# Expert weight places, first loads after an expert stage, and a first panel in halves, in a two-block transformer kernel

## What is computed

```python
def moe(h, router, w_gate, w_up, w_down):            # three times in the program
    combine = top-2 weights of each token over 16 experts
    y = 0
    for e in range(16):
        he = silu(h @ w_gate[e]) * (h @ w_up[e])     # 1024 x 512 each
        y = y + combine[:, e:e+1] * (he @ w_down[e]) # 512 x 1024
    return y

x = x + attention and gate branches;  x = x + cross_attention(x, mem);  x = x + moe(rms_norm(x))
for i in range(2):
    shift, scale, gate = split(silu(c) @ ada_w[i, 0] + ada_b[i, 0])
    y = (stick_breaking, retention)[i](x * (1 + scale) + shift)
    x = layer_norm(alpha * x + (1 + gate) * y)
    ... the same with its own ada weights around moe ...
```

## Time and profile before

| | us |
|---|---|
| median of 3 runs (1449.73 to 1451.45) | 1450.96 |
| the profiled execution's own time | 1445.98 |
| its span on the core | 1444.1 |
| PE busy | 1306.9 (91%) |
| DVE / ACT / POOL busy | 571.7 / 432.8 / 407.8 |
| the load queue's packets, share of 16 engines | 77.9% |
| HBM read | 445.38 MB, 309 GB/s over the span |

### The profile page before, as it was taken

How to read it: one execution, slowest core, us unless ns; L and a number is a source line. 1 busy time by engine, 2 the same in 40 slices (tenths; PEclk the granted TensorE clock), 3 DMA queues, 4 the chain that set the end, 5 groups by cost and what they waited for, 6 DMA issues and landing times.

```text
span 1444.1 us, 20713 instructions
## 1 busy us (share of the span) xinstructions
PE 1306.9 (91%) x7694; PEld 809.8 (56%) x7695; DVE 571.7 (40%) x1234; ACT 432.8 (30%) x693; POOL 407.8 (28%) x190
## 2 busy tenths in 40 slices
PE   6999998889899899998889999699998979998985
PEld 6887787543334388776333344299886853343422
DVE  5598555522112243447223222376007062422224
ACT  4554443211111236443111111145445331111110
POOL 5893544100000067151000000169964710000000
PEclk9999999999999999999999999999999999999998
DMA  9565567899999995429499999986635479999962
GB/s 356 198 223 178 190 234 291 364 407 416 426 428 425 397 357 189 175 66 404 186 392 413 426 428 424 391 324 212 224 117 219 160 321 398 415 426 428 425 247 108
DMA packets 96829, 448.05 MB, mean 310 GB/s; under 512 B 8092, under 2 KB 10056, under 8 KB 77384
## 3 DMA queue, kind: packets, MB, share of 16 engines
q1 hardware_dynamic: 93056, 445.87, 77.9%
q10 hardware_dynamic: 3656, 0.57, 0.2%
HBM read 445.38 MB, written 1.05 MB: 309 GB/s over the span
## 4 chain that ended last, share of the span: by engine, by line
PE 62%; DMA 20%; DVE 9%; issue 3%; ACT 3%; POOL 2%; SPq 1%; DVEq 0%; ACTq 0%; POOLq 0%
PE ps L432 61%; DMA ring_hi<-in_moe_w_up 9%; DMA ring_lo<-in_w_up 8%; DMA ring_lo<-in_ada_w 3%; POOL WLO L2604 1%; SPq L1260 1%; DVE Z L2020 1%; DVE Z L2008 1%; DVE Z L2021 1%; DVE Z L2019 1%; DMA ring_lo<-in_w_ckv 1%; PE ps L454 1%; POOL RS L2573 1%; ACT WHI L1403 0%; PE ps L897 0%
## 5 line engine op out<-in xcount | busy, mean ns | idle before, releaser
L2604 POOL TENSOR_TENSOR WLO<-ring_lo,WHI 128x1024 fp32r<-128x1024 f32 (+1 forms) x154 | 376.9, 2464 | 675.2 <-ACT WHI L1403 673.4
L432 PE MATMUL ps<-ring_lo,Z 128*64 128x512 f32 x1328 | 435.4, 603 | 24.0 <-DMA ring_hi<-in_moe_w_up 5.3
L432 PE MATMUL ps<-ring_hi,Z 128*64 128x512 f32 x1072 | 379.7, 605 | 20.2 <-DMA ring_lo<-in_w_up 7.1
L432 PEld LDWEIGHTS ps<-ring_lo,Z 128*64 128x64 f32 x1328 | 137.8, 138 | 226.3 <-issue 208.2
L1403 ACT ACTIVATE WHI<-ring_lo 128x1024 fp32r<-128x1024 f32 (+1 forms) x160 | 166.3, 1049 | 204.5 <-PE ps L432 191.4
L432 PEld LDWEIGHTS ps<-ring_hi,Z 128*64 128x64 f32 x1072 | 116.0, 139 | 154.1 <-issue 139.3
L2271 DVE TENSOR_TENSOR Z<-ps,Z 64x512 f32<-64x512 f32 x48 | 33.1, 689 | 331.9 <-ACT Z L1610 325.4
L1610 ACT ACTIVATE Z<-ps 64x512 f32<-64x512 f32 x48 | 28.4, 591 | 344.2 <-PE ps L432 344.2
L432 PE MATMUL ps<-WHI,HTH 128*128 128x512 f32 x320 | 126.4, 395 | 5.0 <-DVE HTL L2473 1.6
L432 PE MATMUL ps<-WLO,HTH 128*128 128x512 f32 x320 | 125.1, 391 | 0.0
L432 PE MATMUL ps<-WHI,HTL 128*128 128x512 f32 x320 | 125.1, 391 | 0.0
(11 more groups left out here) (297 smaller groups left out, 1704.2 us busy)
## 6 DMA issues: line engine op xcount, KB each, us to landing
ring_lo<-in_ada_w SPq DMA_DIRECT2D x24, 2048.0 KB, 8.9
ring_lo<-in_moe_w_gate SPq DMA_DIRECT2D x22, 2048.0 KB, 15.8
ring_hi<-in_moe_w_up SPq DMA_DIRECT2D x20, 2048.0 KB, 17.5
ring_lo<-in_moe_w_down SPq DMA_DIRECT2D x15, 2048.0 KB, 16.1
ring_lo<-in_w_up SPq DMA_DIRECT2D x14, 2048.0 KB, 18.4
ring_hi<-in_moe_w_down SPq DMA_DIRECT2D x13, 2048.0 KB, 15.5
ring_lo<-in_ret_w_in SPq DMA_DIRECT2D x12, 2048.0 KB, 10.5
ring_hi<-in_w_gate SPq DMA_DIRECT2D x9, 2048.0 KB, 16.5
```

The costliest lines, as they stand in the source:

```text
L432: return nc.tensor.matmul(o, l, r, start=start, stop=stop, skip_group_check=True)
L2604: nc.gpsimd.tensor_tensor(WLO[:, q, 0:size], slot(r)[:, q * size:(q + 1) * size], WHI[:, q, 0:size].bitcast(F32), ALU.subtract).then_inc(S ...
```

## The change

Four parts.

1. In every pair but the first, odd up and even down change places. Before, from pair 2 on, odd up went where the pair before had its odd up, and even down where it had its even down; now odd up goes where its even down was, and even down where its odd up was. In pair 1 odd up, even down and odd down went to pair 0's odd gate, odd up and even down; now they go to its even down, odd gate and odd up. The waits in `slot_left` follow: odd up waits for the downs of the pair before, even down for the odd gate and up. The order of the loads stays.
2. Behind the first and second expert stage the first `ada` panel is loaded ahead of the first dense panel. ACT copies its result first, and splits the dense panel's quarters 0 and 1 before the turned rows and 2 and 3 behind them.
3. `ckv` 0 is loaded in two halves with a semaphore each, and ACT waits for the half that it needs.
4. In `layer_norm` the gate product of the piece (t 1, h 0) stands ahead of the wait for the power of t 0 instead of behind the normalised row.

```diff
     ADA_AFTER = {("in", "gb1"): (0, 1), ("w_out", 0): (2, 3), ("cq", 0): (4, 5, 6), ("co", 0): (7, 8, 9),
-                 ("sb", 0): (10, 11), ("sb", 5): (12, 13), ("sb_out", 1): (14, 15, 16, 17),
-                 ("ret", 0): (18, 19), ("ret", 10): (20,), ("ret", 11): (21,), ("ret_out", 3): (22, 23)}
+                 ("moe", 0): (10,), ("sb", 0): (11,), ("sb", 5): (12, 13), ("sb_out", 1): (14, 15, 16, 17),
+                 ("moe", 1): (18,), ("ret", 0): (19,), ("ret", 10): (20,), ("ret", 11): (21,), ("ret_out", 3): (22, 23)}
...
-        first, odd = s[:6], [s[6]] + s[:5]
-        even = odd[:2] + [s[5]] + odd[3:]
+        first, odd = s[:6], [s[6], s[0], s[1], s[4], s[2], s[3]]
+        even = [s[6], s[0], s[5], s[2], s[4], s[3]]
...
+    first_in = [S("half_even"), landed[place[("ckv", 0), 0][0]]]
+    HALVES_BEFORE = (16, 0)
...
-                load(place[key, 0][0], *src)
+                if key == ("ckv", 0):
+                    to = slot(place[key, 0][0]).rearrange("p (c n) -> p c n", n=512)
+                    for h in range(2):
+                        c = slice(KC // 2 * h, KC // 2 * h + KC // 2)
+                        sp.dma_start(to[:, c], src[0][:, c]).then_inc(first_in[h], 16)
+                else:
+                    load(place[key, 0][0], *src)
...
-                if (a, j) == (1, 1):
+                if (a, j) == (0, 2):
                     blocks(L, e - 1, 1)
...
+                elif (a, j) == (1, 1):
+                    wait_expert_read(L, e - 2, 0, 2)
+                elif (a, j) == (0, 2):
+                    wait_expert_read(L, e - 1, 1, 1)
...
+                else:
+                    act.wait_ge(first_in[q // 2], 16)
...
-            split_next(("sb", 0))
             ada_copy(10)
+            split_next(("sb", 0), parts=(0, 1))
             turn_split("sbx", KC)
+            split_next(("sb", 0), parts=(2, 3))
             ada_copy(11)
...
+            def gated(t, h):
+
+                o = result(dve, (*key, t, h))
+                link(V.tensor_tensor(o, o, GB[:, 512 * h:512 * h + 512], ALU.mult))
+                return o
...
-                rstd(row_moments(t, EPS_LN, False))
+                k = row_moments(t, EPS_LN, False)
+                if t == 0:
+                    gated(1, 0)
+                rstd(k)
```

More of the change, by code:

```diff
@@ L981, in pair @@
                     if final:
-                        pe.wait_ge(S(("half_even", "half_odd")[a]), 32 * (L + 1))
+                        pe.wait_ge(S(("half_even", "half_odd")[a]), HALVES_BEFORE[a] + 32 * (L + 1))
                     for j in range(0 if final else 2):
@@ L1395, in split_next @@
             r, landed_at, _ = place[key, 0]
-            act.wait_ge(landed[r], landed_at)
+            if n:
+                act.wait_ge(landed[r], landed_at)
             size = stream[order.index(key)][1][1] // QUARTERS
@@ L1750, in _ @@
         if ("ret", 0) in order:
-            split_next(("ret", 0))
             ada_copy(18)
+            split_next(("ret", 0), parts=(0, 1))
             turn_split("rx", KC)
+            split_next(("ret", 0), parts=(2, 3))
             ada_copy(19)
@@ L2402, in layer_norm @@
             key = ("sb_out" if s == 0 else "ret_out", "o")
+            def gated(t, h):
+                o = result(dve, (*key, t, h))
+                link(V.tensor_tensor(o, o, GB[:, 512 * h:512 * h + 512], ALU.mult))
+                return o
             for t in range(NT):
                 for h in range(2):
-                    o = result(dve, (*key, t, h))
-                    link(V.tensor_tensor(o, o, GB[:, 512 * h:512 * h + 512], ALU.mult))
+                    o = result(dve, (*key, 1, 0)) if (t, h) == (1, 0) else gated(t, h)
                     v = X[:, t, 512 * h:512 * h + 512]
```

## The result

The changed kernel took 1482.68 us (median of 4 runs, 1482.15 to 1483.45) against 1450.59 for the kernel before in the same comparison: ratio 1.0227, 95% interval 1.0211 to 1.0244, so 30.6 to 35.4 us slower. The forecast was +21.2, and the time lies 1.7 us above the range; +32.9 is even 0.6 above the sum of all its upper bounds (+32.3). The sign was as forecast, and so was the largest cost, the exchange of places; the size of the whole was not. (All times are medians at the usual speed; one execution of the kernel with the wait in pair 2 took 3370.5 us and is left out.)

A forecast was written before the change was run, and what follows sets the result against it. Expert stages were taken to run at the load queue's rate, one panel per 4.95 us. Terms 13.2 + 7.2 + 3 + 0 - 2.2 + 0 = +21.2 us on 1450.96 gave 1472.2 us, range 1459 to 1481.

The forecast's parts named there:

- the exchange of places: Expert stages: later issue of odd up costs +13.2 us at pair 2, +7.2 at the even pairs behind pairs 3 and 5.

The follow-up runs named there:

- the kernel with the wait in pair 2: Kernel before with its own places; SP's odd up additionally waits for the downs of the pair before, in pair 2 of each stage only: 1456.60 us, ratio 1.0057.

## What to carry to other kernels

When a load is made to wait longer, find the first place where the queue empties, not only the first place where an engine waits: the debt is passed on to the next bound landing. Delays on the same queue don't add: a load that is late behind landings that are late already costs little. When a piece of elementwise work is moved on one engine, look at what its neighbour does at the new time, and follow the chain one stage past the point at which the move was aimed. And where two waits end within a few us of each other, removing one is worth only the distance to the next; here PE waited 3.5 us for the third panel instead.

## What the runs showed of the hardware

DVE and POOL hold each other up. DVE instructions with two SBUF inputs of 128x1024 take 1.22 us alone and 3.3 to 3.4 us beside POOL's quarters of some 2.35 us (1.22 + 2.35 = 3.6, an estimate, if each waits for one of the other's); one with a PSUM input (128x512) keeps its 0.69. POOL's own quarters go from 2.33 each (6.98 for 3) to 3.28 (16.40 for 5). The Trainium skill, "SBUF — State Buffer", section "SBUF: two separate sides", has the rule: the two engines share a port pair that one instruction holds to its end while the other waits. The trace agrees, and the rule should have been asked of the held-back quarters.

DMA loses 0.8 us (median) at a load that is issued with 3.0 to 4.2 us of landings left in the queue, although a panel takes 4.95 there; the counts stand under "What a margin is worth".
